# First norm's scale and shift folded into the router, a shorter expert selection, the first expert gathered ahead of the branch, page loads in groups, index keys on two queues

## What is computed

```python
for i in range(DEPTH):                                    # 2 layers, one router for both
    h, ... = mixer_a(x, past k, v pages) if i == 0 else mixer_b(x, past k, v, index-key pages)
    x = layer_norm(ALPHA * x + h, ln_g[i, 0], ln_b[i, 0])               # the first norm
    x = layer_norm(ALPHA * x + moe(x), ln_g[i, 1], ln_b[i, 1])
    x = x + sigmoid(x @ ple_gate_w[i] + ple_gate_b[i]) * (p[i] @ ple_proj[i])

def moe(t):                                               # 16 experts in 4 groups of 4
    aff = sigmoid(t @ router_w);  sel = aff + router_b
    g = argmax over groups of (sum of the two largest sel in the group)
    idx = the two largest sel inside group g
    gate = aff[idx] / sum(aff[idx])
    return sum over e of combine[:, e] * (silu(t @ w_gate[e]) * (t @ w_up[e])) @ w_down[e]
```

## Time and profile before

| | |
|---|---|
| median of 3 runs (lowest to highest) | 1365.01 us (1361.35 to 1365.46) |
| the profiled execution: time / span | 1363.73 us / 1361.9 us |
| PE busy / DVE / ACT / POOL | 1196.2 us (88%) / 475.4 (35%) / 340.0 (25%) / 47.3 (3%) |
| chain that ended last, by engine | PE 68%, DVE 9%, DMA 9%, SP's queue 7%, issue 4%, ACT 3% |
| DMA moved | 360.29 MB, mean 265 GB/s |
| page stage, expert entry 0, index keys, expert entry 1 | about 127 to 320, 356 to 401, 676 to 755, 984 to 1028 us of the span |

### The profile page before, as it was taken

How to read it: one execution, slowest core, us unless ns; L and a number is a source line. 1 busy time by engine, 2 the same in 40 slices (tenths; PEclk the granted TensorE clock), 3 DMA queues, 4 the chain that set the end, 5 groups by cost and what they waited for, 6 DMA issues and landing times.

```text
span 1361.9 us, 19003 instructions
## 1 busy us (share of the span) xinstructions
PE 1196.2 (88%) x6635; PEld 597.6 (44%) x6636; DVE 475.4 (35%) x1035; ACT 340.0 (25%) x773; POOL 47.3 (3%) x81
## 2 busy tenths in 40 slices
PE   7999998988859999999498798998939999999856
PEld 3445666554423333333246445555433333333333
DVE  1011655552531011111534598365261111111263
ACT  1112545452102111211112414654011111211110
POOL 1200000001000000000100000000100000000101
PEclk9999999998869999999799899999958999999978
DMA  9935699979309799999531744335624989999721
GB/s 331 359 139 186 234 383 360 384 293 384 141 16 376 308 393 429 425 422 420 162 122 32 254 120 136 101 100 226 264 94 191 389 314 428 424 424 425 283 74 39
DMA packets 97278, 360.29 MB, mean 265 GB/s; under 512 B 17024, under 2 KB 35488, under 8 KB 75952
## 3 DMA queue, kind: packets, MB, share of 16 engines
q1 hardware_dynamic: 88528, 328.79, 62.2%
q0 software_dynamic: 5984, 21.59, 4.8%
q10 hardware_dynamic: 2688, 8.91, 1.7%
HBM read 341.48 MB, written 17.78 MB: 264 GB/s over the span
## 4 chain that ended last, share of the span: by engine, by line
PE 68%; DVE 9%; DMA 9%; SPq 7%; issue 4%; ACT 3%; DVEq 0%; POOL 0%; POOLq 0%; ACTq 0%
PE PS L874 15%; PE PS L597 13%; PE PS L895 8%; PE PS L847 7%; PE PS L1022 4%; DMA ring<-in_moe_w_up 3%; SPq L360 3%; DMA ring<-in_cache_a_k 3%; PE PS L1003 3%; PE PS L722 3%; SPq L449 2%; PE PS L856 2%; PE PS L884 1%; PE PS L672 1%; PE PS L877 1%
## 5 line engine op out<-in xcount | busy, mean ns | idle before, releaser
L874 PE MATMUL PS<-ring,QKV 128*64 128x512 f32 (+1 forms) x512 | 231.1, 600 | 6.6 <-ACT QKV L1336 3.9
L877 PE MATMUL PS<-ring,QKV 128*64 128x512 f32 (+1 forms) x512 | 231.0, 600 | 0.0
L1336 ACT ACTIVATE QKV<-PS 128x512 f32<-128x512 f32 (+5 forms) x180 | 95.0, 528 | 399.3 <-PE PS L847 110.0
L597 PE MATMUL PS<-ring,XT 128*64 128x256 f32 (+1 forms) x576 | 150.1, 482 | 3.2 <-DMA ring<-in_a_w_in 2.6
L874 PEld LDWEIGHTS PS<-ring,QKV 128*64 128x64 f32 (+1 forms) x512 | 71.7, 142 | 152.3 <-issue 148.2
L895 PE MATMUL PS<-ring,QKV 128*64 128x512 f32 (+1 forms) x512 | 123.8, 599 | 0.0
L847 PE MATMUL PS<-X,QKV 128*64 128x512 f32 x432 | 103.7, 616 | 15.7 <-issue 15.7
L597 PEld LDWEIGHTS PS<-ring,XT 128*64 128x64 f32 (+1 forms) x576 | 71.0, 162 | 82.4 <-issue 72.3
L2005 DVE TENSOR_TENSOR QKV<-QKV,PS 64x512 f32<-64x512 f32 (+1 forms) x32 | 21.7, 679 | 233.6 <-ACT QKV L1511 233.6
L2010 DVE COPY QKV<-PS 64x512 f32<-64x512 f32 (+1 forms) x32 | 22.2, 692 | 189.2 <-PE PS L895 189.2
L1003 PE MATMUL PS<-ring,XT 128*128 128x512 f32 (+1 forms) x256 | 74.2, 504 | 7.7 <-ACT XT L1336 7.7
(11 more groups left out here) (311 smaller groups left out, 1301.3 us busy)
## 6 DMA issues: line engine op xcount, KB each, us to landing
ring<-in_moe_w_gate SPq DMA_DIRECT2D x32, 2048.0 KB, 11.8
ring<-in_moe_w_up SPq DMA_DIRECT2D x32, 2048.0 KB, 16.1
ring<-in_moe_w_down SPq DMA_DIRECT2D x32, 2048.0 KB, 13.8
ring<-in_cache_a_k SPq DMA_DIRECT2D x64, 512.0 KB, 7.2
ring<-in_cache_a_v SPq DMA_DIRECT2D x64, 512.0 KB, 6.6
ring<-in_a_w_in SPq DMA_DIRECT2D x5, 2048.0 KB, 25.6
ring<-in_ple_gate_w SPq DMA_DIRECT2D x4, 2048.0 KB, 13.2
ring<-in_cache_b_k SPq DMA_DIRECT2D x64, 128.0 KB, 2.0
```

What stands on the lines that cost most here:

```text
L597: ins = pe.matmul(PS[p0:p1, banks[u % 4], 0:c1 - c0], rows_of(k, t), wt[:, k, c0:c1], start=(k == 0), stop=(k == KD - 1))
L874: ins = pe.matmul(PS[0:m, 0, :], XE[:, k, 0:m], wg[:, k, :], start=(k == 0), stop=(k == KD - 1))
L877: ins = pe.matmul(PS[p1:p1 + m, 1, :], XE[:, k, 0:m], wu[:, k, :], start=(k == 0), stop=(k == KD - 1))
L1336: ins = act.activation(dst, src, ACT.Copy) if scale is None else \
```

## The change

There are five parts.

1. **Pages in groups of four.** `LOADS` writes out an order of 32 groups (key or value, batch, half). `page_groups()` gives each group a ring slot: the first six take slots 0 to 5 in turn, every later one takes the slot of the next group to be used up. PE waits for whole groups. `past_values` is cut 4 and 5 instead of 5 and 4, and both cuts count in `pv_mm`.
2. **Router on the normalised rows.** The norm becomes `norm_tokens`: the normalised rows go to `XH`, a part of `QKV`, and PE turns those for the router. The gain is multiplied into the router weights (`FOLDED`), the shift becomes a column `ROUTER_BIAS` (a first set of matmuls, `column_sums` with one moving column), which ACT adds when it copies the sums. Scale and shift of `X` itself stand behind the normalise of all tiles, but for tile 0. ACT runs an unused sigmoid ahead of the real one.
3. **Shorter selection.** The sum of the two largest of four is taken as a maximum over pair sums; one mask instruction goes; the gate weights are computed behind the mask, and constants `before` and `place` are shifted by one so that two later instructions go.
4. **First expert ahead of the branch.** `select` for expert 0 (in two halves), `rows`, both copies and `turn` stand in front of the branch; the counts get a semaphore step of their own, and the row numbers are made after `COUNT`.
5. **Index keys on two queues.** SP issues batches 0 to 3, POOL batches 4 to 7, behind the gather and ahead of `spread`.

```diff
+LOADS = [("k", 1, 1), ("k", 0, 1), ("k", 1, 0), ("v", 0, 0), ("k", 0, 0), ("v", 0, 1), ("k", 2, 0)]
+for _b in range(1, DB):
+    LOADS += [("v", _b, 0), ("v", _b, 1)] + [("k", _b + 1, 1)] * (_b + 1 < DB) + [("k", _b + 2, 0)] * (_b + 2 < DB)
+def freed(what, b, g):
+    return ("score_mm", 3 * b + g + 1) if what == "k" else ("pv_mm", 2 * b + g + 1)
+def page_groups():
+    used = [(what, b - (what == "v"), g) for b in range(DB + 1) for what in "vk" for g in range(2)
+            if 0 <= b - (what == "v") < DB]
+    slot, load, last, count = {}, {}, {}, [0] * SLOTS
+    for i, group in enumerate(LOADS):
+        s = i if i < SLOTS else slot[used[i - SLOTS]]
+        count[s] += 1
+        slot[group], load[group], last[s] = s, count[s], group
+    return slot, load, [freed(*group) for group in used], [freed(*last[s]) for s in range(SLOTS)]
...
             def page_turn(b, j):
-                pe.wait_ge(k_landed[j], b * 16 + 16)
+                if j % 4 == 0:
+                    pe.wait_ge(pages_landed[group_slot["k", b, j // 4]], 64 * group_load["k", b, j // 4])
...
             def router(layer):
...
+                pe.wait_ge(*at(f"router_landed{layer}", 48))
+                pe.wait_ge(*at(f"aff_ones{layer}", 1))
+                pe.wait_ge(*at(f"out_evac{layer}", 4))
+                column_sums(SMF, lambda k: SHIFT_T[:, k:k + 1], 7, 3 * NE, 1)
+                turn_tile(0, 1)
+                turn_tile(1, 3)
+                scores(0)
+                turn_tile(2, 4)
+                scores(1)
+                scores(2)
...
+            def experts(layer):
+                pe.wait_ge(*at(f"sel_ready{layer}", 1))
+                pe.wait_ge(*at(f"normed{layer}0", 6))
+                rows(layer, 0, 0, 4).then_inc(S(f"rows_mm{layer}"), 1)
+                pe.wait_ge(*at(f"dispatch_ready{layer}", 1))
+                most = pe.value_load(COUNT[0:1, NE:NE + 1], min_val=0, max_val=TOK)
                 pe.wait_ge(*at(f"pt_evac{layer}", 1))
+                pe.wait_ge(*at(f"rows_evac{layer}", 1))
+                turn(5).then_inc(S(f"xe_mm{layer}"), 1)
                 with pe.If(most > 128):
...
+            def norm_tokens(layer, tile):
...
+                tile(0)
+                normalise(0, normed)
+                scale(0, normed, 1)
+                tile(1)
+                normalise(1, normed)
+                tile(2)
+                normalise(2, normed)
+                ve.memset(G[:, 0, :], 1.0).then_inc(S(f"aff_ones{layer}"), 1)
+                scale(1, normed, 3)
+                scale(2, normed, 4)
...
                 first_of_max(g3(5), code, mx, g3(7), NE)
                 link(ve.tensor_tensor(g3(8), g3(6), g3(7), ALU.add))
-                link(ve.tensor_tensor(g3(9), g3(8), g3(0), ALU.mult))
+                ve.memset(G[NS:P, 8, 32:48], 0.0).then_inc(S(f"mask_ready{layer}"), 1)
...
+                ve.wait_ge(*at(f"pos_mm{layer}", 1))
+                before = PS[:, 3, 0:48].rearrange("p (t e) -> p t e", t=3)
+                link(ve.tensor_tensor(WHERE[:, 0:3 * NE].rearrange("p (e t) -> p t e", t=3), before, g3(8), ALU.mult))
+                for half in range(2):
+                    select(layer, 0, 0, 64 * half, 64 * half + 64)
...
-                    for b in range(DB):
+                    for b in range(DB // 2):
...
+                    for b in range(DB // 2, DB):
+                        for j in range(NPAGE):
+                            pg = pool.value_load(pt_sb[0:1, bass.ds(b * NPAGE + j, 1)], min_val=0, max_val=pool_pages - 1)
+                            pool.dma_start(kx[:, b // 2, j, b % 2, :],
+                                           cache_b_kidx[0, bass.ds(pg, 1)].rearrange("a p d -> (a p) d"))\
+                                .then_inc(S("late_keys_landed"), 16)
```

More of the change, by code:

```diff
@@ L784, in router, with column_sums @@
             def router(layer):
-                pe.wait_ge(*at(f"out_evac{layer}", 6))
-                pe.wait_ge(*at(f"router_landed{layer}", 16))
-                for t, (t0, n) in enumerate(TILES):
-                    transposed(layer, "router", lambda t, k: half_chunk(X, t, k),
-                               lambda t: pe.wait_ge(*at(f"normed{layer}0", t + 1)), (t,), done=2 * t)
-                    pe.wait_ge(*at(f"turn{layer}_evac", TURNED[layer]["router"] + 2 * t + 2))
+                def column_sums(weights, moving, bank, c0, n):
                     for round in range(2):
@@ L817, in positions, with rows @@
                                     start=(t == 0), stop=(t == 2))
                 ins.then_inc(S(f"pos_mm{layer}"), 1)
+            def rows(layer, par, places, bank, release=False):
+                for t in range(3):
+                    for half in range(2):
+                        ins = pe.matmul(PS[64 * half:64 * half + 64, bank, :], SEL[:, par, t, places:places + 64],
+                                        X[:, t, 512 * half:512 * half + 512], start=(t == 0), stop=(t == 2))
+                        if release and t == 0 and half == 0:
+                            ins.then_inc(S(f"experts_used{layer}"), 2)
+                return ins
@@ new lines, in turn @@
+            def turn(bank):
+                for k in range(4):
+                    ins = pe.transpose(PS[:, bank, k * 128:k * 128 + 128],
+                                       XR.rearrange("p (f k) -> p k f", k=4)[:, k, :], ident)
+                return ins
+            def experts(layer):
[4 more added lines that the diff above has]
+                most = pe.value_load(COUNT[0:1, NE:NE + 1], min_val=0, max_val=TOK)
@@ L841, in slot_of @@
                     return ring[:, s, :]
-                def rows(par, places, bank, release=False):
-                    for t in range(3):
-                        for half in range(2):
-                            ins = pe.matmul(PS[64 * half:64 * half + 64, bank, :], SEL[:, par, t, places:places + 64],
-                                            X[:, t, 512 * half:512 * half + 512], start=(t == 0), stop=(t == 2))
-                            if release and t == 0 and half == 0:
-                                ins.then_inc(S(f"experts_used{layer}"), 2)
-                    return ins
-                def turn(bank):
-                    for k in range(4):
-                        ins = pe.transpose(PS[:, bank, k * 128:k * 128 + 128],
-                                           XR.rearrange("p (f k) -> p k f", k=4)[:, k, :], ident)
-                    return ins
                 def expert(i, par, e, m):
@@ L897, in expert @@
                     ins.then_inc(S(f"sp_y_mm{layer}"), 1)
-                pe.wait_ge(*at(f"sel_ready{layer}", 1))
-                rows(0, 0, 4).then_inc(S(f"rows_mm{layer}"), 1)
-                pe.wait_ge(*at(f"rows_evac{layer}", 1))
-                turn(5).then_inc(S(f"xe_mm{layer}"), 1)
                 with pe.Fori(0, NE // 2) as i:
@@ L1465, in _, with norm_root @@
                     copy(dst, src, "so_t0_evac", small[:, 3:4])
-            def norm_root(layer, which):
-                for t in range(3):
+            def norm_root(layer, which, tiles=(0, 1, 2)):
+                for t in tiles:
                     act.wait_ge(*at(f"var{layer}", 3 * which + t + 1))
@@ L1544, in experts_dense @@
             def experts_dense(layer):
+                for k in range(KD):
+                    ins = act.activation(XT[:, k, :], XT[:, k, :], ACT.Identity, bias=SHIFT_T[:, k:k + 1],
+                                         scale=GAIN_T[:, k:k + 1])
+                ins.then_inc(S(f"ht_evac{layer}"), 2)
                 act.wait_ge(*at(f"acc_zero{layer}", 1))
-                act.sem_inc(S(f"ht_evac{layer}"), 2)
                 with act.Fori(0, NE // 2) as i:
@@ L2106, in gated_input @@
                 ve.wait_ge(*at(f"gated{layer}", 6))
-            norm(0, 0, residual(0))
+            norm_tokens(0, residual(0))
             experts(0)
@@ L2246, in _ @@
             sample_outputs(DB - 1)
-            norm(1, 0, residual(1))
+            norm_tokens(1, residual(1))
             experts(1)
```

264 lines of the change are left out of this document (149 added, 115 removed).

## The result

The changed kernel takes 1325.29 us (median of 4 runs, 1323.91 to 1329.33) against 1365.24 (4 runs, 1361.35 to 1366.53): a ratio of 0.9717, 95% interval 0.9688 to 0.9746, faster. The prediction was 1322 us, 1308 to 1340. The profiled execution took 1325.06 us, with a span of 1323.4.

The account below looks back on a forecast made before the run. PE was taken to wait long in three places: page stage, expert entry and index keys. Gains of 10.7 + 21.4 + 10.2 = 42.3 us from 1363.7 gave 1321.4, a median of about 1322 us, range 1308 to 1340.

Parts of the forecast that it names:

- Pages, 10.7: Page stage: six batch pitches fall from 22.53 to 20.74 us, gaining 10.7; bounds 0 and 12.8.
- Rival A: Page stage: pages stay bound by DMA, the pages term goes and the time is 1333 us; chance 0.13.
- The two bounds, 20.74 for PE and 20.4 for DMA: Page stage: a batch takes the longer of PE's work, 20.74 us, and DMA's 16 pages at 411 GB/s, 20.4.
- Norm and router, 6.4: Expert entry: DVE's selection starts at 369.3 where it was 375.74, gaining 6.4 us.
- selection, 1.5: Expert entry: 26 instructions instead of 33 up to the mask, 5.55 us instead of 7.05.
- First expert ahead of the branch, from 18.2 between mask and gate matmul to 14.9: Expert entry: with the mask at 374.9, the first gate matmul comes at 389.8 against 401.00, 11.2 us earlier.
- The branch: Expert entry: PE's branch isn't hidden behind the turn; before, from `COUNT` to rows took 5.29 us.
- its bounds of 385.1 and 390.4: Expert entry: first gate matmul at 385.1 if PE's branch is hidden, 390.4 at the upper bound; 389.8 taken.
- The clock, 0.5 back in each entry: Expert entry: first gate matmuls start at half clock, 2 us lost against 1.4 before; net 0.5, bounds +1.4 and -4.
- An entry: Expert entry of one layer, all terms: 10.7 us gained, bounds 6.6 and 17.3; both layers 21.4.
- Index keys, 10.2: Ahead of the key turn: the 8.5 us wait goes and the transposes lose 1.7; 10.2 gained, bounds 0 and 10.3.
- rivals C and D: Index keys: POOL's pages late, over 2.6 us each, 1332 us (C, 0.05); over 3.8, slower, 1401 at 5 (D, 0.02).

Follow-up runs that it names:

- the run with the rows put back: Changed kernel with the first expert's rows, copy, turn and copy put back behind the branch on PE and ACT: 1326.67 us, ratio 0.9731.
- the exchanged branches: Changed kernel with PE's two branches in the other order, sparse experts right behind the test, dense ones behind them: 1314.34 us, ratio 0.9655.
- entry alone: Kernel before with only the folded norm, shorter selection and first expert ahead of the branch: 1343.01 us, ratio 0.9862.
- everything together: Changed kernel with PE's branches swapped, 48 index pages on SP and 16 on POOL, and idle matmuls ahead of mask and gate: 1312.45 us, ratio 0.9634.

## Why the prediction was right

The time was 3 us above the forecast and inside its range. Page stage, entry and index keys each gained what the prediction said, by the mechanism that it gave, but for the first expert's gather. That the total came out so near is in part luck: 6.0 us of losses that no term foresaw met some 2 us of gains that none foresaw either. By its own terms, against the profile:

- **Pages, 10.7.** Six pitches of 20.66 for a forecast 20.74: 11.2. Rival A, pages that DMA still holds up, is out: no landing is on the chain, and DMA held 404 GB/s from the first of these pitches to the last. The two bounds, 20.74 for PE and 20.4 for DMA, lie so close that the pitch by itself can't tell them apart.
- **Norm and router, 6.4; selection, 1.5.** 6.5 and 1.55. DVE ended last, as argued: ACT's sigmoid was over at 356.18, DVE's norm at 358.09.
- **First expert ahead of the branch, from 18.2 between mask and gate matmul to 14.9.** 15.03 in layer 0. The size is right and the name of the part is wrong: 2.2 us of the 3.2 come from the count, copied 3.23 us behind the mask instead of 5.39, since the row numbers are made after it. Moving the rows gave 1.2 at the gate matmul, and half of that or less at the second rows (the run with the rows put back).
- **The branch.** The prediction took it as exposed, by the 5.29 of the same branch before: 5.71 and 4.29. This choice decided between its bounds of 385.1 and 390.4 for the gate matmul, which came at 389.74 in the frame of the kernel before, forecast 389.8. Why the branch costs that much the prediction left open; the exchanged branches show it. The Trainium skill, Runtime: NRT & Kernel Launch, section "Instruction fetch mechanics", says that a taken branch whose target isn't in the window of fetched pages stalls for a fetch; the trace agrees, with a packet on q8 inside the wait of 5.71 us and none where the wait is 1.06.
- **The clock, 0.5 back in each entry.** 0.64 in layer 0 (gate matmul to second `rows` 9.23 us, 8.59 before), nothing in layer 1. An entry: 10.6 and 11.9, forecast 10.7. Layer 1 gained 1.3 more than layer 0: its branch waits 1.4 us less and the clock takes 0.6 less, while the first rows take 0.8 longer.
- **Index keys, 10.2.** 10.3 at the key turn. POOL's page took 1.13 us, forecast 1.5, its nearest row being 0.96; rivals C and D needed 2.6 and 3.8.
- **What it left out** is a price for POOL's transfers behind the time of their issue. POOL's 36 more transfers cost 3.0 us at the end of the program, behind everything that the prediction looked at. Without them the profiled execution would stand at 1322. The 3.0 us between the experts and layer 1 (gather and clock) were not foreseen either.

That the parts add up is shown only roughly. Alone they give 6.8, 6.9 and 20.6 us by their medians, 34.3 together against 40.0; the four intervals together allow for about 7 us. The branch's price, the clock at single places and the gather move by 1 to 3 us each from one build to the next, and none of them is work that the change adds or takes away.

## What to carry to other kernels

Write the code that runs right behind the test and leave the jump to the end of the stage, where another wait hides it: here that was worth more than gathering work ahead of the branch, which only moved the wait. When a step is put in front of a wait, ask what the wait is for, and price the move as if the wait stayed. When issues are spread over engines, look also at the end of the program, behind the last store, for what each queue costs there.

## What the runs showed of the hardware that was not expected

- The same branch on PE kept it idle for 4.94 to 7.04 us between the turn and the gate matmul (changed kernel and entry alone), and for 1.70 when the code that runs followed directly. With the branch right behind the count, PE needed 5.43 us from the count to the rows in the kernel before and 7.60 with the page groups alone, whose edit stands in another stage; q8 moved one packet in the first wait and two in the second. What decides how many are fetched isn't shown.
- Each transfer issued by POOL added 0.083 us between the last store and the end of the span (0 more: 8.98 and 8.99; 4: 9.35; 20: 10.65; 32: 11.62; 36: 11.97).
- With everything together the granted clock was 1.00 under the counts and fell to half within the rows (0.62 over all of them), when PE had stood for 0.78 us and 0.31 us shortly before. With the sparse experts first it was 1.00 through PE's waits behind the rows and under the gate matmuls in layer 0; in layer 1 it was 0.98 through the same waits, and the gate matmuls started at half.
